# Grouped heads of a two-layer hybrid backbone: the second map is turned behind the first slot of filler, its product comes behind the second

## The chip, the cores and the metric

The kernel runs on one core of a Trainium2 chip. The core has a matrix engine (TensorE; PE in the rows, PEld its weight load), VectorE (DVE), ScalarE (ACT), GpSimd (POOL) and SyncE (SP), which issues the DMAs. Each engine runs its own list of instructions in order and waits at semaphores for the others. The metric is the device time of one execution in microseconds, as the median of several runs.

## The reference

Two layers over 512 latent and 256 context tokens of width 1024. Each layer normalises, projects once into the inputs of three branches, runs them, merges them with gates and adds a gated feed-forward block. What matters here is branch A, attention with eight query heads and two key heads:

```
def gqa_attend(q, k, v):
    s = jnp.einsum('bqkgd,btkd->bkgqt', q * ATTN_SCALE, k).astype(jnp.float32)
    p = jax.nn.softmax(s, axis=-1).astype(v.dtype)
    return jnp.einsum('bkgqt,btkd->bqkgd', p, v)
```

Latent queries attend to all 768 keys (context and latent), context queries to the 256 context keys alone. Branch B is differential attention with four heads (two softmax maps, one subtracted from the other), branch C a convolution. In the second layer only the latent queries are needed.

## The kernel before, in words

**Numbers.** Every value that enters a matrix product is split into a high part, rounded for the matrix engine, and a low part, the rest. A product is three matmuls (high by high, high by low, low by high; L477, L478, L479). ScalarE writes the high part, VectorE (or, for weights, GpSimd) the low one.

**Heads and items.** Attention runs over eight "heads": j = 0 to 3 are grouped heads, each a pair of two query heads, whose two softmax maps lie side by side; j = 4 to 7 are the differential heads. A head runs over query tiles of 128 rows: six in layer 0 (four latent ones with 768 keys, then two context ones with 256 keys), four in layer 1. One query tile of one head is an item, g; `i` is its number within the head.

**What an item does.** `scores` (L576, matmuls at L586) writes the two maps to `sco0` and `sco1`. VectorE takes each map's maximum (`maximum`, L1224, into NM). ScalarE takes the exponential into M with the row sum (`exp`, `ACTIVATE M<-sco,NM`). VectorE scales by the reciprocal of the sum (`gqa_probs`, L1243 and L1244). TensorE turns the probabilities with transposes (`turn_probs`, L599), three blocks of 128 at a time, into the two PSUM banks `aux0` and `aux1`; a context item needs one bank for each map. ScalarE copies the high part out of the bank (`turned_hi`, `ACTIVATE RB<-aux`), VectorE the low part (`turned_lo`, L1181 `RB<-aux,RB`), and only with the latter is the bank free again. `weigh` (L603) is the product with the values for both maps together, 18 matmuls for 768 keys into the bank `acc1`; ScalarE copies the result out (`ACTIVATE X<-acc`, two of 64 rows).

**Filler.** Between these steps TensorE works on the input projection of the next head, in chunks of three matmuls (L477 to L479, `acc<-H,WHI` and `WLO`) into the bank `acc0`; eight chunks make one tile of 384 columns (layer 0) or 512 (layer 1). Each item has two slots of filler, `slot(j, 2 * i)` and `slot(j, 2 * i + 1)`. The table FILL (L47) says how many chunks each slot holds:

```
    (0, "gqa"): [3, 3, 2, 3, 3, 2, 3, 3, 2, 3, 2, 3],
    (1, "gqa"): [4, 4, 2, 2, 1, 1, 1, 1],
    (0, "diff"): [8, 4, 4, 8, 4, 4, 8, 4, 4, 8, 4, 4],
    (1, "diff"): [8, 8, 8, 4, 4, 8, 4, 4],
```

The kind is that of the next head, so head 3 runs with the "diff" rows. To a slot belongs more than the chunks. Where a tile ends in it, ScalarE evacuates the bank in its own slot of the same number (`ACTIVATE M<-acc` or `U<-acc`), and with the last tile of a kind it also splits the next weight tile (`hi`, L788). Some slots later come the sums of squares of each head row (`head_sums`, L564, which also use the two aux banks), their logarithm and exponential on ScalarE (`ACTIVATE R<-aux`, `R<-R`), the rotation on VectorE (`rope`, L1190 and three L1181), its scaling (`normed`), and the split of the new queries and keys (`normed_hi`, `normed_lo`).

**What sets the order.** The order is written out by hand in three loops over the items, one for each engine: TensorE's at L619, ScalarE's at L883, VectorE's at L1273. The three agree in which slot a piece of work falls. The scores of item g+1 are issued right behind the first turn of item g, so that its softmax runs on VectorE and ScalarE while TensorE does the rest of item g.

Of the kernel before, what the change touches and what calls it, by code (L numbers as in the profile page):

```python
# [26 lines left out]
P = 128  # L27
# [102 lines left out]
def build(nc, xT, vecs, consts, wdw, w_mod, w_in, w_gate, w_br, w_out, w_fi, w_fo, out):  # L130
    x_next = nc.dram_tensor("x_next", (P, KC, LAT), F32).ap()

    with ExitStack() as ctx:
# [302 lines left out]
        def _(pe):  # L436
# [139 lines left out]
            def scores(l, g, j, q, k0):  # L576

                kv = kv_buffer(j)
                u = c.at("sc")
                pe.wait_ge(S("exp"), u)  # L580
                pe.wait_ge(S("qk"), qk_count(l, j))
                for a, w, o in ([(0, LAT, 0), (LAT, CTX, LAT)] if k0 == 0 else [(LAT, CTX, 0)]):
                    for n, (x, y) in enumerate(((0, 0), (0, 1), (1, 0))):
                        for m in range(2):
                            h = slice(m * HEAD, m * HEAD + HEAD)
                            mm = nc.tensor.matmul(sco[m][:, o:o + w], QB[h, j % 2, x, q:q + P], KB[h, kv, y, a:a + w],  # L586
                                                  start=n == 0, stop=n == 2)
                            if n == 2 and (k0 or a):
                                mm.then_inc(S(f"scored{m}"), 1)
                c.step("sc")  # L590
# [28 lines left out]
            def attention(l):  # L619
                items = attention_items(l)  # L620
                n = n_tok(l)
                parts = lambda k0: 2 if k0 == 0 else 1

                def project(j):
                    for t, rngs in next_tiles(l, j):
                        yield from tile_chunks((l, j, t), rngs)

                def slot(j, s):
                    if j + 1 == HEADS:
                        return  # L630
                    for _ in range(FILL[l, kind_of(j + 1)][s]):
                        next(chunks)
                    ends = last_slots(l, j + 1)
                    uses = lambda t: [at[(l, j + 1, t), r] for r in range(len(dict(next_tiles(l, j + 1))[t]))]
                    if s == ends["q"] + 1:
                        head_sums(0, n, (l, j + 1, "qs"), uses("q"))
                    if j + 1 >= 4 and s == ends["k"] + 1:
                        head_sums(1, TOK, (l, j + 1, "ks"), uses("k"))
                    if j + 1 >= 4 and s == ends["v"] + 1:
                        turn_v((l, j + 1, "vt"), uses("v"))  # L640

                scores(l, 0, *items[0][0:1], *items[0][2:4])
                for g, (j, i, q, k0) in enumerate(items):
                    if i == 0 and j + 1 < HEADS:
                        chunks = project(j + 1)
                    after = items[g + 1] if g + 1 < len(items) else None
                    turn_probs((l, g, 0), 2 * (g % 2), k0)
                    if after:
                        scores(l, g + 1, after[0], after[2], after[3])
                    if j < 4:  # L650
                        turn_probs((l, g, 1), 2 * (g % 2) + 1, k0)
                    slot(j, 2 * i)
                    if g and items[g - 1][0] >= 4 and items[g - 1][1] % 2:
                        sub_sums((l, g - 1, "ss"), at[l, g - 1, "o"])
                    if i == 0:
                        wait_free("aux", *(at[(l, 0 if j < 4 else j, "vt"), a] for a in range(2)))
                    if j < 4:
                        weigh((l, g, "o"), j, k0, [at[(l, g, m), p] for m in range(2) for p in range(parts(k0))])
                    elif i % 2:
                        weigh((l, g, "o"), j, k0, [at[(l, e, 0), p] for e in (g - 1, g) for p in range(parts(k0))])  # L660
                    slot(j, 2 * i + 1)
                sub_sums((l, g, "ss"), at[l, g, "o"])
                at["attention", l] = dict(c.n)

# [91 lines left out]
        def _(act):  # L756
# [126 lines left out]
            def attention(l):  # L883
# [45 lines left out]
                for g, (j, i, q, k0) in enumerate(items):  # L929
                    after = items[g + 1] if g + 1 < len(items) else None  # L930
                    turned_hi((l, g, 0), 0 if j < 4 else P * (i % 2), k0)
                    if j < 4:
                        turned_hi((l, g, 1), P, k0)
                    if after:
                        exp(0, g + 1, after[3])
                        exp(1, g + 1, after[3])
                        if after[0] >= 4:
                            weighted(g + 1, after[3])
                    slot(j + 1, 2 * i)
                    if j < 4:  # L940
                        b = take(at[l, g, "o"])
                        for m in range(2):
                            rows = slice(m * HEAD, m * HEAD + HEAD)
                            fn(X[rows, j, q:q + P], acc[b][rows, m * P:(m + 1) * P], ACT.Copy,
                               sem=f"acc_free{b}" if m else "oraw")
                    elif i % 2:
                        b = take(at[l, g, "o"])
                        fn(X[:, j, q - P:q + P], acc[b][:, 0:256], ACT.Copy, sem="oraw")
                        fn(OSQ, acc[b][:, 0:256], ACT.Square, sem=f"acc_free{b}")
                    if g and items[g - 1][0] >= 4 and items[g - 1][1] % 2:  # L950
                        sub_factor(l, g - 1)
                    slot(j + 1, 2 * i + 1)
                sub_factor(l, g)
                c.n.update((k, at["attention", l][k]) for k in ("acc", "aux"))

# [209 lines left out]
        def _(dve):  # L1165
# [107 lines left out]
            def attention(l):  # L1273
# [28 lines left out]
                for g, (j, i, q, k0) in enumerate(items):  # L1302
                    after = items[g + 1] if g + 1 < len(items) else None
                    turned_lo((l, g, 0), 0 if j < 4 else P * (i % 2), k0)
                    if after:
                        maximum(0, g + 1, after[3])
                    if j < 4:
                        turned_lo((l, g, 1), P, k0)
                    if after:
                        maximum(1, g + 1, after[3])  # L1310
                    if after and after[0] < 4:
                        gqa_probs(g + 1, after[3])
                    elif after:
                        diff_factors(l, g + 1)
                    slot(j + 1, 2 * i)
                    if after and after[0] >= 4:
                        diff_probs(g + 1, after[3])
                    if g and items[g - 1][0] >= 4 and items[g - 1][1] % 2:
                        sub_norm(l, g - 1, items[g - 1][0], items[g - 1][2])
                    slot(j + 1, 2 * i + 1)  # L1320
# [335 lines left out]
```

## Time and profile before

| | us |
|---|---|
| median of 3 runs (lowest, highest) | 2765.39 (2762.3, 2768.44) |
| the profiled execution | 2768.71 |
| its span | 2766.8 |
| TensorE busy | 2485.3 (90%) |
| VectorE, ScalarE, GpSimd busy | 1214.9, 1150.5, 1019.4 |

Times in the rows are microseconds from the start of the span. A row of the timeline gives start, duration, engine, line and operation, the tile written and those read, the shape and a count; behind it, in brackets, for how long the engine had been idle and what released it. Neighbouring instructions of one kind are merged into one row, with the count. A row of the stretches gives, for each engine, busy time and number of instructions, then the granted clock of TensorE (1.00 is 2.4 GHz, 0.50 is 1.2 GHz), the DMA engines' share and GB/s.

### The profile page before, as it was taken

Reading aid. Unit: us, or ns where it says so; the run is one execution under the profiler, and the core shown is the slowest. Engines: PE = TensorE matmul, PEld = TensorE weight load, DVE = VectorE, ACT = ScalarE, POOL = GpSimd, SP = SyncE. Lnnn points to the kernel's source line nnn. Section 1 sums busy time; section 2 is a strip of 40 time slices with the busy share of each in tenths; the row PEclk is TensorE's granted clock in tenths of the full one; section 3 lists DMA queues with packets and bytes.
Section 4 is the critical chain, followed back from the end, with each engine's and each line's share of the span. In section 5 each row is a group of like instructions: output and inputs, shape, how many; then the busy total and the mean of one; then the engine's idle time right before and its main releaser. Section 6 shows DMA issues by size and latency. Waiting matters only on the chain.

```text
span 2766.8 us, 34285 instructions
## 1 busy us (share of the span) xinstructions
PE 2485.3 (90%) x13556; PEld 2211.2 (80%) x13556; DVE 1214.9 (44%) x1810; ACT 1150.5 (42%) x2256; POOL 1019.4 (37%) x771
## 2 busy tenths in 40 slices
PE   5999888789988998999999998888877869899998
PEld 2888777679987997999999996777666657688887
DVE  3566555578994233111111125764457982311111
ACT  4555566643334335322331226655653233432222
POOL 1201111058883533544552232111113535444443
PEclk9999999889998998999999998999988989999999
DMA  5100111023332422332332121111101214233332
GB/s 203 51 24 24 31 31 39 12 72 120 119 116 80 163 77 69 107 99 77 115 101 68 58 73 61 31 31 38 39 16 54 84 50 133 78 98 99 99 92 91
DMA packets 62077, 209.02 MB, mean 76 GB/s; under 512 B 7392, under 2 KB 7648, under 8 KB 61664
## 3 DMA queue, kind: packets, MB, share of 16 engines
q1 hardware_dynamic: 61920, 206.84, 23.8%
q8 instruction: 109, 1.79, 0.3%
q14 instruction: 48, 0.39, 0.0%
HBM read 202.62 MB, written 4.19 MB: 75 GB/s over the span
## 4 chain that ended last, share of the span: by engine, by line
PE 45%; DVE 10%; ACT 5%; issue 1%; POOL 0%; ACTq 0%; DVEq 0%
PE acc L477 14%; PE acc L478 14%; PE acc L479 14%; DVE X L1491 5%; ACT M L792 2%; DVE M L1181 2%; DVE RB L1181 1%; PE sco L536 1%; PE aux L599 1%; ACT H L792 1%; DVE NM L1224 1%; ACT WHI L788 1%; PE sco L586 1%; ACT RB L792 1%; ACT R L792 0%
## 5 line engine op out<-in xcount | busy, mean ns | idle before, releaser
L401 POOL TENSOR_TENSOR WLO<-STG,WHI 128x512 fp32r<-128x512 f32 (+1 forms) x760 | 1015.4, 1362 | 1724.2 <-ACT WHI L788 1724.1
L477 PE MATMUL acc<-H,WHI 128*128 128x384 f32 (+2 forms) x2528 | 926.3, 366 | 94.8 <-ACT M L792 44.2
L478 PE MATMUL acc<-H,WHI 128*128 128x384 f32 (+2 forms) x2528 | 904.2, 358 | 0.0
L479 PE MATMUL acc<-H,WLO 128*128 128x384 f32 (+2 forms) x2528 | 903.3, 357 | 0.0
L788 ACT ACTIVATE WHI<-STG 128x512 fp32r<-128x512 f32 (+1 forms) x760 | 410.3, 591 | 628.3 <-PE acc L479 405.7
L477 PEld LDWEIGHTS acc<-H,WHI 128*128 128x128 f32 x2528 | 488.8, 193 | 155.7 <-issue 66.6
L479 PEld LDWEIGHTS acc<-H,WLO 128*128 128x128 f32 x2528 | 489.5, 194 | 33.6
L478 PEld LDWEIGHTS acc<-H,WHI 128*128 128x128 f32 x2528 | 490.5, 194 | 30.2
L1491 DVE SCALAR_TENSOR_TENSOR X<-U,WDW,X 128x783 f32<-128x783 f32 (+1 forms) x256 | 336.7, 1315 | 14.8 <-ACT X L792 6.9
L477 PE MATMUL acc<-RB,WHI 128*128 128x384 f32 (+1 forms) x816 | 291.8, 358 | 24.0 <-DVE T L1181 11.2
L1181 DVE TENSOR_TENSOR T<-G,acc 128x384 f32<-128x384 f32 (+1 forms) x114 | 68.2, 599 | 528.2 <-PE acc L479 524.6
L479 PE MATMUL acc<-RB,WLO 128*128 128x384 f32 (+1 forms) x816 | 288.7, 354 | 0.0
L478 PE MATMUL acc<-RB,WHI 128*128 128x384 f32 (+1 forms) x816 | 288.6, 354 | 0.0
L1181 DVE TENSOR_TENSOR RB<-aux,RB 128x384 fp32r<-128x384 f32 (+1 forms) x236 | 119.2, 538 | 228.0 <-ACT RB L792 226.7
L1401 DVE SCALAR_TENSOR_TENSOR X<-acc,MOD,X 128x384 f32<-128x384 f32 (+1 forms) x128 | 67.5, 549 | 320.7 <-PE acc L479 320.7
L477 PEld LDWEIGHTS acc<-RB,WHI 128*128 128x128 f32 x816 | 153.7, 188 | 44.1 <-DVE T L1181 14.1
L792 ACT ACTIVATE M<-sco,NM 128x768 f32<-128x768 f32 (+1 forms) x160 | 129.8, 814 | 85.6 <-DVE NM L1224 85.6
L479 PEld LDWEIGHTS acc<-RB,WLO 128*128 128x128 f32 x816 | 153.8, 188 | 10.9
L599 PE MATMUL aux<-K,M 128*128 128x128 f32 x624 | 101.0, 296 | 68.1 <-DVE M L1257 30.6
L478 PEld LDWEIGHTS acc<-RB,WHI 128*128 128x128 f32 x816 | 153.8, 188 | 10.1
L599 PEld LDWEIGHTS aux<-K,M 128*128 128x128 f32 x624 | 75.7, 150 | 90.9 <-issue 45.1
L792 ACT ACTIVATE RB<-aux 128x384 fp32r<-128x384 f32 (+1 forms) x236 | 102.6, 477 | 102.5 <-PE aux L599 99.8
(112 smaller groups left out, 2352.4 us busy)
## 6 DMA issues: line engine op xcount, KB each, us to landing
STG<-in_w_fi SPq DMA_DIRECT2D x88, 512.0 KB, 3.5
STG<-in_w_mod SPq DMA_DIRECT2D x80, 512.0 KB, 3.5
STG<-in_w_in SPq DMA_DIRECT2D x52, 512.0 KB, 3.5
STG<-in_w_gate SPq DMA_DIRECT2D x48, 512.0 KB, 3.5
STG<-in_w_fo SPq DMA_DIRECT2D x32, 512.0 KB, 3.5
STG<-in_w_br SPq DMA_DIRECT2D x48, 256.0 KB, 2.6
FIRST<-in_w_mod SPq DMA_DIRECT2D x8, 1024.0 KB, 18.6
STG<-in_w_out SPq DMA_DIRECT2D x16, 512.0 KB, 3.6
```

The costliest lines, as they stand in the source:

```text
L401: nc.gpsimd.tensor_tensor(WLO[:, s, a:a + w], STG[:, g, a:a + w], WHI[:, s, a:a + w].bitcast(F32), ALU.subtract).then_inc(S("w_split"), 1)
L477: nc.tensor.matmul(dst, lh, rh, start=first, stop=False)
L478: nc.tensor.matmul(dst, lh, rl, start=False, stop=False)
L479: return nc.tensor.matmul(dst, ll, rh, start=False, stop=last)
L536: mm = nc.tensor.matmul(sco[0][:, row:row + MOD_GROUP], SCX[:, 4 * (4 * q + k):4 * (4 * q + k) + P], w[:, s, k * MOD_GROUP:(k + 1) * MOD_G ...
L586: mm = nc.tensor.matmul(sco[m][:, o:o + w], QB[h, j % 2, x, q:q + P], KB[h, kv, y, a:a + w], start=n == 0, stop=n == 2)
L599: t = nc.tensor.transpose(dst[:, n * P:(n + 1) * P], PR[:, slot, (k - k0) * P:(k - k0 + 1) * P], IDENT)
L788: nc.scalar.activation(WHI[:, s, a:a + w], STG[:, g, a:a + w], ACT.Copy).then_inc(S("w_hi"), 1)
L792: ins = nc.scalar.activation(dst, src, f, **kw)
L1181: return nc.vector.tensor_tensor(dst, a, b, op)
L1401: nc.vector.scalar_tensor_tensor(X[:, j, s:s + m], acc[b][:, s - a:s - a + m], MOD[:, l, part, j, st:st + 1], X[:, j, s:s + m], ALU.mult, ...
L1491: own("tap", nc.vector.scalar_tensor_tensor(o, u, wt, o, ALU.mult, ALU.add))
```

## The change

In the items of heads 0 to 3 each of the three loops is written in another order. On TensorE the second map's turn moves from ahead of the first slot to behind it, the second slot moves ahead of the product. On ScalarE the copies of the second turn move from ahead of the two exponentials to behind the first slot's work, and the copy of the product's result moves behind the second slot's. On VectorE the low parts of the second turn move from between the two maxima to behind the scaling of the next item's probabilities and the first slot's work. Differential heads keep their order.

```
@@ TensorE, attention
                     turn_probs((l, g, 0), 2 * (g % 2), k0)
                     if after:
                         scores(l, g + 1, after[0], after[2], after[3])
+                    slot(j, 2 * i)
                     if j < 4:
                         turn_probs((l, g, 1), 2 * (g % 2) + 1, k0)
-                    slot(j, 2 * i)
+                        slot(j, 2 * i + 1)
...
                         weigh((l, g, "o"), j, k0, [at[(l, e, 0), p] for e in (g - 1, g) for p in range(parts(k0))])
-                    slot(j, 2 * i + 1)
+                    if j >= 4:
+                        slot(j, 2 * i + 1)
@@ ScalarE, attention
                     turned_hi((l, g, 0), 0 if j < 4 else P * (i % 2), k0)
-                    if j < 4:
-                        turned_hi((l, g, 1), P, k0)
                     if after:
                         exp(0, g + 1, after[3])
                         exp(1, g + 1, after[3])
...
                     slot(j + 1, 2 * i)
                     if j < 4:
+                        turned_hi((l, g, 1), P, k0)
+                        slot(j + 1, 2 * i + 1)
                         b = take(at[l, g, "o"])
...
-                    slot(j + 1, 2 * i + 1)
+                    if j >= 4:
+                        slot(j + 1, 2 * i + 1)
@@ VectorE, attention
                     turned_lo((l, g, 0), 0 if j < 4 else P * (i % 2), k0)
                     if after:
                         maximum(0, g + 1, after[3])
-                    if j < 4:
-                        turned_lo((l, g, 1), P, k0)
                     if after:
                         maximum(1, g + 1, after[3])
...
                     slot(j + 1, 2 * i)
+                    if j < 4:
+                        turned_lo((l, g, 1), P, k0)
                     if after and after[0] >= 4:
                         diff_probs(g + 1, after[3])
```

TensorE's list at item 2 of a head of layer 1, before; `aux<-K,M` are the turns, `sco<-RB` the next item's scores, `acc<-H` filler, `acc<-RB` the product:

```order
L599 MATMUL aux<-K,M 128x128 x6
L586 MATMUL sco<-RB 128x512 x6
L586 MATMUL sco<-RB 128x256 x6
L599 MATMUL aux<-K,M 128x128 x6
L477 MATMUL acc<-H,WHI 128x512
L478 MATMUL acc<-H,WHI 128x512
L479 MATMUL acc<-H,WLO 128x512
L477 MATMUL acc<-RB 128x256
```

The same place now:

```order
L599 MATMUL aux<-K,M 128x128 x6
L586 MATMUL sco<-RB 128x512 x6
L586 MATMUL sco<-RB 128x256 x6
L477 MATMUL acc<-H,WHI 128x512
L478 MATMUL acc<-H,WHI 128x512
L479 MATMUL acc<-H,WLO 128x512
L599 MATMUL aux<-K,M 128x128 x6
L477 MATMUL acc<-H,WHI 128x512
L478 MATMUL acc<-H,WHI 128x512
L479 MATMUL acc<-H,WLO 128x512
L477 MATMUL acc<-RB 128x256
```

The second turn has one slot on either side, and the product follows the second slot.

ScalarE's list at items 2 and 3 of head 0 of layer 0, before; `RB<-aux` are the copies of turned blocks (two for each map), `M,L<-sco,NM` the exponentials, `X<-acc` the product's result, `WHI<-STG` the weight split:

```order
L792 ACTIVATE RB<-aux 128x3x128 x4
L792 ACTIVATE M,L<-sco,NM 128x768 x2
L792 ACTIVATE X<-acc 64x128 x2
L792 ACTIVATE M<-acc,EC,V 128x384
L792 ACTIVATE M<-acc 128x384
L788 ACTIVATE WHI<-STG 128x512 x2
L792 ACTIVATE RB<-aux 128x3x128 x4
```

The same place now:

```order
L794 ACTIVATE RB<-aux 128x3x128 x2
L794 ACTIVATE M,L<-sco,NM 128x768 x2
L794 ACTIVATE RB<-aux 128x3x128 x2
L794 ACTIVATE M<-acc,EC,V 128x384
L794 ACTIVATE M<-acc 128x384
L790 ACTIVATE WHI<-STG 128x512 x2
L794 ACTIVATE X<-acc 64x128 x2
L794 ACTIVATE RB<-aux 128x3x128 x2
```

The four copies have become two ahead of the exponentials and two behind them, and `X<-acc` stands last in its item.

VectorE's list over one item with 768 keys on both sides, before; `RB<-aux,RB` are the low parts, `NM<-sco` the maxima, `M<-M,RL` the scalings:

```order
L1181 TENSOR_TENSOR RB<-aux,RB 128x3x128 x2
L1224 TENSOR_REDUCE NM<-sco 128x1
L1181 TENSOR_TENSOR RB<-aux,RB 128x3x128 x2
L1224 TENSOR_REDUCE NM<-sco 128x1
L1243 RECIPROCAL RL<-L 128x1
L1244 TENSOR_SCALAR M<-M,RL 128x768
L1243 RECIPROCAL RL<-L 128x1
L1244 TENSOR_SCALAR M<-M,RL 128x768
```

The same place now, with the item behind it:

```order
L1227 TENSOR_REDUCE NM<-sco 128x1 x2
L1246 RECIPROCAL RL<-L 128x1
L1247 TENSOR_SCALAR M<-M,RL 128x768
L1246 RECIPROCAL RL<-L 128x1
L1247 TENSOR_SCALAR M<-M,RL 128x768
L1184 TENSOR_TENSOR RB<-aux,RB 128x3x128 x4
L1227 TENSOR_REDUCE NM<-sco 128x1 x2
```

The low parts of the second turn now come behind both scalings, next to the first two of the item that follows.

## Rows read from the trace of the kernel before

**Rows 1.** The page, busy time of each engine

```profile
PE 2485.3 (90%) x13556; PEld 2211.2 (80%) x13556; DVE 1214.9 (44%) x1810; ACT 1150.5 (42%) x2256; POOL 1019.4 (37%) x771
```

**Rows 2.** Stretches, heads 0 to 2 of layer 0 and layer 1; PEclk before the DMA columns

```profile
108.85:253.64 144.79, 131.63 (x901) 116.73 (x901) 92.36 (x191) 84.47 (x209) 12.49 (x10) 0.98 0.07 23
1714.00:1823.84 109.84, 97.73 (x654) 82.22 (x655) 74.17 (x141) 64.95 (x149) 12.53 (x10) 0.98 0.09 28
```

**Rows 3.** Waits of TensorE, heads 0-3: layer 0, then layer 1; total, times, longest

```profile
PE aux L599 <- DVE RB L1181: 11.8, 8, 2.0
...
PE aux L599 <- DVE RB L1181: 10.1, 11, 1.6
PE acc L477 <- DVE RB L1181: 4.7, 6, 0.8
```

**Rows 4.** Stretches, items of head 2 of layer 0, then of head 1 of layer 1

```profile
206.09:215.21 9.12, 8.22 (x62) 7.47 (x60) 5.44 (x11) 5.66 (x14) 2.51 (x2) 1.00 0.17 57
215.21:223.89 8.68, 7.98 (x59) 7.00 (x58) 5.34 (x10) 4.98 (x12) 0.00 (x0) 1.00 0.01 2
223.89:231.54 7.65, 7.65 (x59) 6.99 (x57) 5.34 (x10) 4.16 (x10) 0.00 (x0) 1.00 0.00 0
231.54:242.29 10.75, 8.71 (x59) 7.72 (x58) 7.25 (x16) 7.32 (x17) 2.49 (x2) 1.00 0.16 51
242.29:248.24 5.95, 4.90 (x33) 4.13 (x32) 3.41 (x9) 3.33 (x10) 0.00 (x0) 1.00 0.00 0
248.24:253.64 5.40, 5.40 (x39) 4.64 (x37) 3.77 (x8) 3.18 (x8) 0.00 (x0) 1.00 0.00 0
...
1750.66:1762.10 11.44, 10.50 (x67) 8.87 (x66) 5.15 (x10) 5.76 (x14) 2.51 (x2) 1.00 0.16 48
1762.10:1772.28 10.18, 8.63 (x60) 7.37 (x59) 6.83 (x14) 7.72 (x17) 2.50 (x2) 1.00 0.17 52
1772.28:1779.94 7.66, 6.60 (x49) 5.40 (x48) 7.18 (x14) 4.63 (x11) 0.00 (x0) 1.00 0.00 0
1779.94:1787.24 7.30, 6.49 (x50) 5.42 (x49) 5.48 (x11) 4.16 (x11) 0.00 (x0) 1.00 0.01 2
```

**Rows 5.** Timeline, item 2 of head 1 of layer 0, three engines

```profile
174.88 0.82 PE L599 MATMUL aux<-K,M 128*128 128x128 f32 x6
...
175.93 1.02 DVE L1181 TENSOR_TENSOR RB<-aux,RB 128x384 fp32r<-128x384 f32 x2 [2.87 <-ACT RB L792]
...
176.87 0.88 PE L599 MATMUL aux<-K,M 128*128 128x128 f32 x6
176.98 0.96 DVE L1224 TENSOR_REDUCE NM<-sco 128x1 f32<-128x768 f32 x1
...
178.22 0.91 ACT L792 ACTIVATE M<-sco,NM 128x768 f32<-128x768 f32 x1
...
179.26 0.36 PE L477 MATMUL acc<-RB 128*128 128x256 f32 x1
...
179.97 0.62 DVE L1244 TENSOR_SCALAR M<-M,RL 128x768 f32<-128x768 f32 x1
...
181.69 0.57 ACT L792 ACTIVATE X<-acc 64x128 f32<-64x128 f32 x2 [0.79 <-PE acc L479]
```

**Rows 6.** Timeline, work of the slots: evacuation, rotation, head sums, key split

```profile
172.11 0.66 ACT L792 ACTIVATE M<-acc,EC,V 128x384 f32<-128x384 f32 x1
...
190.00 0.72 DVE L1190 STREAM_SHUFFLE G<-M 128x512 f32<-128x512 f32 x1
190.63 1.23 ACT L792 ACTIVATE R<-aux,EC 128x384 f32<-128x384 f32 x2 [1.13 <-PE aux L564]
...
1779.40 0.68 DVE L1181 TENSOR_TENSOR RB<-M,RB 128x512 fp32r<-128x512 f32 x1
```

**Rows 7.** Stretches, behind two idle times of 2.04 us in layer 0

```profile
138.00:140.00 2.00, 2.00 (x8) 2.00 (x7) 1.79 (x6) 1.27 (x5) 0.00 (x0) 0.51 0.63 162
236.50:239.00 2.50, 2.50 (x14) 1.97 (x13) 2.26 (x9) 1.66 (x6) 0.00 (x0) 1.00 0.66 216
```

More of the change, by code:

```diff
@@ L649, in attention @@
                         scores(l, g + 1, after[0], after[2], after[3])
+                    slot(j, 2 * i)
                     if j < 4:
                         turn_probs((l, g, 1), 2 * (g % 2) + 1, k0)
-                    slot(j, 2 * i)
+                        slot(j, 2 * i + 1)
                     if g and items[g - 1][0] >= 4 and items[g - 1][1] % 2:
@@ L660, in attention @@
                         weigh((l, g, "o"), j, k0, [at[(l, e, 0), p] for e in (g - 1, g) for p in range(parts(k0))])
-                    slot(j, 2 * i + 1)
+                    if j >= 4:
+                        slot(j, 2 * i + 1)
                 sub_sums((l, g, "ss"), at[l, g, "o"])
@@ L931, in attention @@
                     turned_hi((l, g, 0), 0 if j < 4 else P * (i % 2), k0)
-                    if j < 4:
-                        turned_hi((l, g, 1), P, k0)
                     if after:
@@ L940, in attention @@
                     if j < 4:
+                        turned_hi((l, g, 1), P, k0)
+                        slot(j + 1, 2 * i + 1)
                         b = take(at[l, g, "o"])
@@ L951, in attention @@
                         sub_factor(l, g - 1)
-                    slot(j + 1, 2 * i + 1)
+                    if j >= 4:
+                        slot(j + 1, 2 * i + 1)
                 sub_factor(l, g)
@@ L1306, in attention @@
                         maximum(0, g + 1, after[3])
-                    if j < 4:
-                        turned_lo((l, g, 1), P, k0)
                     if after:
@@ L1315, in attention @@
                     slot(j + 1, 2 * i)
+                    if j < 4:
+                        turned_lo((l, g, 1), P, k0)
                     if after and after[0] >= 4:
```

## The prediction, made before the result was known

> **What bounds the kernel now.** TensorE has work in 90% of the span [rows 1], and the page's clock row stands at 8 to 9 tenths nearly throughout, so I read the change as a question about TensorE's idle time in the grouped heads and nothing else. The order of views was: the page, then the time by stretches to find these heads, then the waits of TensorE inside them, then one item in order of time.
>
> The change touches heads 0 to 3 of both layers. Heads 0 to 2 take 144.79 us in layer 0 and 109.84 us in layer 1 [rows 2]; head 3, whose filler is that of a differential head, comes on top. In layer 0's grouped heads TensorE waits 11.8 us at the turns for VectorE's split of the turned probabilities, in layer 1's 10.1 us there and 4.7 us at the product for the same kind of split [rows 3]. The first two, 21.9 us in all, are the prize: the second turn needs the two aux banks that the first turn has filled. The reader should see in [rows 4] that not every item pays them: the third item of a layer 0 head takes 7.65 us and TensorE is busy for 7.65 of them, while item 0 of that head holds 0.90 of idle time (9.12 less 8.22) and item 3 holds 2.04 (10.75 less 8.71).
>
> I number items of a head from 0 (six in layer 0, four in layer 1), and count time from the start of an item's first turn.
>
> **What the item does before.** From [rows 5], for item 2 of layer 0: first turn 0, VectorE's two splits 1.05 to 2.07, second turn 1.99 (so the scores of the next item end there), first maximum 2.10 to 3.06, first exponential 3.34, product 4.38, first scaling of the next item's probabilities 5.09 to 5.71, the product's result copied from 6.81 (0.20 behind the product's end at 6.61), next first turn 7.65. Two things matter. The product starts 2.39 us behind the second turn. And ScalarE's copy and VectorE's split of the second turn lie ahead of the exponentials, so nothing but two splits stands between turn and product.
>
> **The change part by part.** Nothing is added or taken away: the same matmuls, copies and splits run. Three orders change.
>
> 1. TensorE: filler, second turn, filler, product, where it was second turn, filler, product, filler. The wait for the aux banks goes: at 1.99 + 1.6 for three chunks the first split (2.07) is long over. Worth up to 21.9 us.
>
> 2. ScalarE: the copy of the second turn now stands behind both exponentials and behind the first slot's work. 3. VectorE: its split stands behind both maxima, both reciprocals and scalings and the first slot's work. Both engines run their list in order (in [rows 5] the exponential starts at 178.22, 0.28 behind the end of its maximum: the copies of the second turn stand ahead of it), so the product now waits for the softmax of the next item, which it does not need.
>
> The chain with the durations of [rows 5], for an item with no extra work in its first slot. The copy of the product's result (0.57 us, at the product's end plus 0.20) now stands directly ahead of the next first turn's copy, which costs that one 0.2. So: splits 1.25 to 2.27; maxima back to back, 2.30 and 3.17, ready 3.26 and 4.12; exponentials 3.29 and 4.18 (0.89 apart, as ScalarE issues them); copies of the second turn from 5.07, first half done 5.55; VectorE scaling 5.40 to 6.02, then the splits 5.94 to 6.96; product 7.2 (0.26 from a split's end to a matmul); product 2.23 long; next first turn 9.4. TensorE itself would be there after 1.99 + 2.39 + 1.04 = 5.4 us, so it waits 1.8. The chain is as long whatever the filler is, so each item now lasts max(chain, TensorE's work).
>
> **Layer 0, heads 0 to 2**, against the undisturbed head in [rows 4]:
> - item 0: chain 9.4 against 9.12, +0.3 (its 0.90 of idle time goes, 1.3 come)
> - item 1: the evacuation of a tile, 0.9 us of ScalarE (two instructions, the first in [rows 6]), stands between exponentials and copy, and the second slot waits for that bank; 10.1 against 8.68, +1.4
> - item 2: 9.4 against 7.65, +1.75
> - item 3: short scores for the next item, but the rotary work of 2.78 us (four instructions of about 0.7, the first in [rows 6]) stands ahead of the split, and the second turn now waits for the banks of the head sums (1.23 us of ScalarE, [rows 6]); split ends 8.5, product 8.7, 10.9 against 10.75, +0.2 (the 2.04 of idle time are taken off in this)
> - item 4: the second slot waits for an evacuation which the product used to cover; 6.75 against 5.95, +0.8
> - item 5: scores of the next head's full tile, chain 5.9 + 0.26, product of six matmuls 0.7; 6.9 against 5.40, +1.5
> A head takes 53.5, three 160.5, against 144.79: **+15.7 us**.
>
> **Layer 1, heads 0 to 2** (slots of 4,4,2,2,1,1,1,1 chunks):
> - item 0: TensorE bound, 2.0 + 2.64 + 0.8 + 2.64 + 2.22 = 10.3 against 11.44, -1.1
> - item 1: rotary work ahead of the split, which ends 9.7; 12.2 against 10.18, +2.0
> - item 2: the key split of 0.68 [rows 6] ahead of it; 10.05 against 7.66, +2.4
> - item 3: chain 9.4 against 7.30, +2.1
> A head takes 42.0, three 126.0; the very first item has no wait at its second turn to lose (nothing stands ahead of it) and starts on a slow clock, so its -1.1 falls away: 127.1 against 109.84, **+17.2 us**.
>
> **Head 3 of both layers** has slots of 4 and 8 chunks; there TensorE is the longer side in most items. The stalls at the turn go, an evacuation is exposed in the items where the first slot ends a tile and the product no longer lies between the slots. I put the two heads at -1.6 together; bounds -6 (all stalls go, nothing comes) and +6 (each item pays 0.6).
>
> **TensorE's clock.** This trace shows no item with idle time like the new ones in heads 0 to 2, so I bound it. Of the four idle times of 2.04 us before item 3's second turn in layer 0, three were followed by a stretch at the 1.2 GHz level; the first and the one that was not stand in [rows 7], with a granted clock of 0.51 and 1.00. Two of these lie in the three heads of 144.79 us, which is 2.14 more than three times the 47.55 of the undisturbed head [rows 2, 4], so about 1.1 us each. Behind 1.55 us or less (item 1 of layer 1 holds 10.18 less 8.63) the clock stayed at 1.00 [rows 4]. The new order has two waits of 2 us or more in each of six heads (item 1 and 4 in layer 0; 2 and 3 in layer 1, with 3.7 and 3.1): nothing to 12 x 1.1 = 13 us. Part of a slow stretch falls where TensorE would wait anyway, so I take **+6**.
>
> The Trainium skill ("TensorE: Matmul & The Clock Gate", A second HAM failure mode: psum-queue depth-cycling) says that frequent small idle times between groups of matmuls are enough to make the clock swing. The idle times of 0.90 and 1.55 us with a clock of 1.00 do not bear this out here; by that page the clock term would be above its upper end, which is rival C.
>
> Sum: 15.7 + 17.2 - 1.6 + 6 = +37.3 us. The profiled execution took 2768.7 us (span 2766.8), 3.3 more than the median, so its counterpart would take 2806 and the median 2802.7.
>
> **The rivals.**
> A. Faster: the second turn's copy does not end up behind the exponentials in effect, because filler covers it. Then the 21.9 us of [rows 3] go and nothing comes: 2743.5. For it: these waits are real and the change removes their cause. Against: it decides only where filler from scores to product exceeds 5.2 us; in heads 0 to 2 that holds for one item of ten, item 0 of layer 1. 5%.
> B. Layer 0 breaks even, because its slots of two or three chunks and shorter handovers than mine hide the chain, and only layer 1 pays: 2765.4 + 17 = 2782. For it: my chain leaves TensorE only 1.3 to 1.8 us idle in most layer 0 items, against 3 to 4 in layer 1. Against: durations and handovers are from the same rows. 12%.
> C. The clock falls at every new wait of over 1 us, that is at some 21 of the 30 items of these six heads, and the slow product and turns lie on the chain: 31.3 + 21 x 1.1 = 54, 2820 (2812 to 2832). For it: the three of four. 14%.
> D. No effect: the chain of the product was only moved, and waits swap one for one, 2765. Against: a layer 1 item has 2.4 us of idle to swap and gets over 3. 3%.
>
> **How the numbers follow.** The forecast, 66%, is 2802, its own range 2787 to 2815 (base 24 to 42, clock 0 to 10). The range of 8 in 10 takes in the upper half of B and the lower half of C and leaves A, D and the rest outside: 2780 to 2822. A difference of 0.2%, 5.5 us, is about what a measurement here can tell from none. Slower: 66 + 12 + 14 = 92%. Same: 3%. Faster: 5%.
>
> **What would show it.** Right: the turns wait no longer for VectorE's split in heads 0 to 2 of either layer (0 to 2 us in all, where 21.9 stood); the product waits for it in nearly every item, some 35 to 55 us in all; layer 0's three heads take about 160 us and layer 1's about 127; outside of the grouped heads every stretch is as long as before. The copy of the second turn starts right behind the second exponential. Wrong: a product that starts with the split of the second turn done before the second exponential; items under 8.5 us in items 2 and 3 of layer 1; a total that moved in the differential heads or behind them.

## The result, and the profile after

The changed kernel takes 2815.21 us (median of 4, 2812.24 to 2823.15) against 2765.33 for the kernel before: a ratio of 1.0191, 95% interval 1.0176 to 1.0206, slower by 50 us. The forecast was 2802, the range 2780 to 2822. The profiled execution is the slowest of the four (2823.15, span 2821.2), so its sections add up to 54.4 us over the span before, where the medians differ by 49.9. Two executions timed for the later experiments (6159 us of the kernel before, 9473 us of the last variant) lie far outside of all others and are left out of the ratios.

First the stretches of the trace after, in the columns of [rows 2]: heads 0 to 2 of layer 0, head 3 of layer 0, everything from there to the first turn of layer 1, heads 0 to 2 of layer 1, head 3 of layer 1.

```profile
110.77:273.66 162.89, 136.31 (x900) 119.85 (x901) 92.05 (x191) 84.30 (x211) 13.35 (x11) 0.96 0.07 20
...
273.66:340.10 66.44, 62.17 (x409) 56.26 (x407) 35.91 (x71) 37.59 (x86) 9.45 (x8) 1.00 0.11 33
...
340.10:1729.99 1389.89, 1276.41 (x7337) 1215.41 (x7336) 573.16 (x806) 544.96 (x1040) 609.65 (x442) 0.96 0.26 82
1729.99:1869.73 139.74, 112.25 (x660) 95.45 (x661) 76.43 (x143) 65.81 (x151) 15.12 (x12) 0.87 0.08 25
1869.73:1933.02 63.29, 55.67 (x327) 46.99 (x327) 30.66 (x55) 32.21 (x68) 7.58 (x6) 0.93 0.10 31
```

The same five of the kernel before, cut at the same instructions (the layer 1 stretch of [rows 2] begins 1.6 us behind its first turn, this one begins at it):

```profile
253.64:321.46 67.82, 62.75 (x407) 57.51 (x405) 38.14 (x72) 38.62 (x89) 10.53 (x8) 0.97 0.11 32
...
321.46:1712.39 1390.93, 1279.45 (x7337) 1216.78 (x7337) 574.04 (x807) 545.17 (x1039) 609.41 (x442) 0.96 0.27 82
...
1712.39:1823.84 111.45, 99.34 (x660) 83.50 (x661) 75.10 (x143) 65.48 (x150) 12.53 (x10) 0.97 0.10 29
1823.84:1879.48 55.64, 50.95 (x327) 43.42 (x326) 31.93 (x55) 31.73 (x69) 10.51 (x8) 1.00 0.12 38
```

Layer 0's heads 0 to 2 have 144.79 us in [rows 2]: +18.1. Head 3 of layer 0 is 1.4 shorter, the long middle 1.0 shorter, layer 1's heads 0 to 2 are 28.3 longer and its head 3 is 7.7 longer. The rest, +2.8, lies ahead of the first turn (1.9) and behind the last grouped head (0.9). So nearly all of it is in the grouped heads. Mind the clock column: 0.87 in layer 1 where 0.97 stood. The 111.45 us before hold a first item of 13.16 us with a clock of 0.77; two later runs that begin layer 1 in the order of before took 10.40 us for it. So the 28.3 us may be up to 3 us too small.

The waits of TensorE in these heads (layer 0 from 110.7 to 340, then layer 1 from 1729.99 to 1933.02), to be read against [rows 3]:

```profile
PE acc L477 <- DVE RB L1184: 11.7, 10, 1.6
PE acc L477 <- ACT M L794: 8.8, 6, 2.1
PE acc L477 <- ACT U L794: 5.4, 3, 1.8
PE acc L477 <- issue: 3.9, 4, 1.1
...
PE aux L599 <- DVE RB L1184: 0.3, 1, 0.3
...
PE acc L477 <- DVE RB L1184: 24.0, 9, 3.5
...
PE aux L599 <- ACT R L794: 5.4, 5, 1.7
...
PE aux L599 <- DVE RB L1184: 1.9, 1, 1.9
```

The waits of the turns for VectorE are 0.3 us where layer 0 had 11.8 and 1.9 where layer 1 had 10.1, all in head 3. New in layer 1 are 5.4 us (0.7 before) in which turns wait for ScalarE to free the banks of the head sums. The product (`acc<-RB`, also L477) now waits for VectorE's split: 11.7 us where layer 0 had 1.4, 24.0 where layer 1 had 4.7. The two rows on ScalarE are filler that waits for an evacuation, in items 1 and 4 of layer 0 and in head 3. Three of the four waits called "issue" stand ahead of the product in item 5 of layer 0, 1.14 us each.

One item in order of time, item 2 of head 1 of layer 0, the one of [rows 5], from the first turn at 186.87:

```profile
186.87 0.82 PE L599 MATMUL aux<-K,M 128*128 128x128 f32 x6
187.07 0.57 ACT L794 ACTIVATE X<-acc 64x128 f32<-64x128 f32 x2 [3.35 <-PE acc L479]
...
188.19 1.02 DVE L1184 TENSOR_TENSOR RB<-aux,RB 128x384 fp32r<-128x384 f32 x2 [3.79 <-ACT RB L794]
189.12 1.81 DVE L1227 TENSOR_REDUCE NM<-sco 128x1 f32<-128x768 f32 x2
190.10 0.90 ACT L794 ACTIVATE M<-sco,NM 128x768 f32<-128x768 f32 x1 [1.57 <-DVE NM L1227]
...
190.54 0.82 PE L599 MATMUL aux<-K,M 128*128 128x128 f32 x6
...
191.87 0.86 ACT L794 ACTIVATE RB<-aux 128x384 fp32r<-128x384 f32 x2
...
192.75 1.02 DVE L1184 TENSOR_TENSOR RB<-aux,RB 128x384 fp32r<-128x384 f32 x2
...
194.02 0.36 PE L477 MATMUL acc<-RB 128*128 128x256 f32 x1 [1.60 <-DVE RB L1184]
```

The second turn is issued at 190.54. ScalarE is busy with the exponentials until 191.87, VectorE with the scalings until 192.75, so the copy and the split of that turn follow only then, and the product starts at 194.02, 7.15 us into the item. The prediction had 7.2, with the copy at 5.07 (measured 5.00) and the split at 5.94 (measured 5.88).

### The profile page after: what moved, and what is told of

It reads as the page before. It is cut to its first block, busy times and chain, and to the rows that moved or that the text cites. A ratio compares the mean times of both kernels' runs of the same rounds, so it can differ in the third digit from the quotient of the medians.

```text
span 2821.2 us, 34285 instructions
## 1 busy us (share of the span) xinstructions
PE 2505.0 (89%) x13556; PEld 2226.7 (79%) x13556; DVE 1212.8 (43%) x1810; ACT 1148.6 (41%) x2256; POOL 1019.8 (36%) x771
## 4 chain that ended last, share of the span: by engine, by line
PE 45%; DVE 10%; ACT 6%; issue 1%; ACTq 0%; DVEq 0%
PE acc L477 14%; PE acc L479 14%; PE acc L478 14%; DVE X L1494 5%; ACT M L794 3%; DVE RB L1184 1%; DVE M L1184 1%; PE sco L536 1%; DVE NM L1227 1%; PE aux L599 1%; PE sco L586 1%; ACT H L794 1%; ACT RB L794 1%; ACT R L794 0%; ACT X L794 0%
## 5 line engine op out<-in xcount | busy, mean ns | idle before, releaser
L477 PE MATMUL acc<-H,WHI 128*128 128x384 f32 (+2 forms) x2528 | 930.0, 368 | 108.8 <-ACT M L794 52.5
L477 PEld LDWEIGHTS acc<-H,WHI 128*128 128x128 f32 x2528 | 488.4, 193 | 175.8 <-issue 66.8
L477 PE MATMUL acc<-RB,WHI 128*128 128x384 f32 (+1 forms) x816 | 292.6, 359 | 23.0 <-DVE T L1184 11.2
L477 PEld LDWEIGHTS acc<-RB,WHI 128*128 128x128 f32 x816 | 154.2, 189 | 43.3 <-DVE T L1184 14.2
L479 PEld LDWEIGHTS acc<-RB,WLO 128*128 128x128 f32 x816 | 154.4, 189 | 10.9
L478 PEld LDWEIGHTS acc<-RB,WHI 128*128 128x128 f32 x816 | 154.3, 189 | 10.1
L477 PE MATMUL acc<-RB 128*128 128x256 f32 x312 | 101.9, 327 | 42.4 <-DVE RB L1184 38.5
L794 ACT ACTIVATE RB<-T 128x384 fp32r<-128x384 f32 (+1 forms) x66 | 37.1, 562 | 247.3 <-DVE T L1184 247.3
```

The costliest lines, as they stand in the source:

```text
L477: nc.tensor.matmul(dst, lh, rh, start=first, stop=False)
L478: nc.tensor.matmul(dst, lh, rl, start=False, stop=False)
L479: return nc.tensor.matmul(dst, ll, rh, start=False, stop=last)
L794: ins = nc.scalar.activation(dst, src, f, **kw)
```

## The experiments

Eight kernels ran. Six differ from the kernel before in order alone, two also hold extra matmuls whose results are overwritten. The first three cuts below are shortened to the order of the steps. In those of the last kernels a function returns three values for each item: whether the second turn stands behind the first slot, whether the product stands behind the second (`last`), and where the second turn's copy and split stand (`'old'` as in the kernel before, `'new'` as in the change). In the lists, `turned_hi(g, 1)` is the copy of the second turn of item g, `turned_lo(g, 1)` its split.

### Only the copy and the split moved

```
 ScalarE  turned_hi(g, 0)
-         turned_hi(g, 1)
          exp(0, g + 1); exp(1, g + 1)
+         turned_hi(g, 1)
          slot(j + 1, 2 * i)
 VectorE  turned_lo(g, 0); maximum(0, g + 1)
-         turned_lo(g, 1)
          maximum(1, g + 1); gqa_probs(g + 1)
+         turned_lo(g, 1)
          slot(j + 1, 2 * i)
```

> TensorE's order is that of before (second turn right behind the scores, product between the slots). Only ScalarE's copy and VectorE's split of the second turn are moved: behind both exponentials and both scalings, ahead of the first slot's work. Theory (the product waits for the softmax of the next item, because copy and split stand behind it in ScalarE's and VectorE's lists): slower than before, and slower than the changed kernel, because the second slot no longer stands ahead of the product: per head about +12 us in layer 0 and +9 in layer 1, with the clock's part 2820 to 2860, I say 2840. The wait of the product for VectorE's split rises from 6 us to over 40. Rival (TensorE's own order costs the time: exposed evacuations, the product behind the last slot): no change from before, 2760 to 2775.

Measured: 2864.26 us (2862.29 to 2867.38), ratio 1.0362 (1.0345 to 1.0379): 100 us slower than before, twice the loss of the change, a little above the stated 2860. One item 1 of layer 0, first turn at 182.33:

```profile
184.32 0.88 PE L609 MATMUL aux<-K,M 128*128 128x128 f32 x6
...
187.19 0.87 ACT L819 ACTIVATE RB<-aux 128x384 fp32r<-128x384 f32 x2
188.06 1.02 DVE L1218 TENSOR_TENSOR RB<-aux,RB 128x384 fp32r<-128x384 f32 x2
189.34 0.36 PE L487 MATMUL acc<-RB 128*128 128x256 f32 x1 [3.07 <-DVE RB L1218]
```

The second turn is where it was, at 1.99 us, and the product starts at 7.01 (4.38 before). With TensorE's list untouched, the place of copy and split in the other two lists alone makes the wait. The rival that TensorE's own order makes the whole loss, with no change from before here, does not stand. That the loss is larger than that of the change fits the second slot: it stands behind the product here and hides nothing of the wait, which is 3.07 us in this item and 1.60 in item 2 above. The waits for VectorE at the product sum to 24.8 us in heads 0 to 2 of layer 0 and 24.9 in those of layer 1, within the "over 40" of the expectation.

### Only the product moved

```
 TensorE  slot(j, 2 * i)
+         slot(j, 2 * i + 1)
          weigh(g)
-         slot(j, 2 * i + 1)
 ScalarE  slot(j + 1, 2 * i)
+         slot(j + 1, 2 * i + 1)
          X <- acc
-         slot(j + 1, 2 * i + 1)
```

> Only the product moves, behind the second slot, in heads 0 to 3; the second turn, its copy and its split stay where they were before. Theory: this part of the change costs little; it exposes an evacuation in items 1 and 4 of layer 0 (+2.1 and +0.7 a head) and in head 3, and hides most of the 0.8 us at the product in items 2 and 3 of layer 1 (-4 in all): +8 us against before, 2765 to 2780. Rival (the order of TensorE's list carries the loss of 50 us): 2800 or more.

Measured: 2771.45 us, ratio 1.0025 (1.0014 to 1.0036), inside the 2765 to 2780. The sum hides two parts of opposite sign. Items 0 to 3 of a layer 1 head, and item 1 of a layer 0 head (columns as in [rows 4]):

```profile
1759.89:1770.92 11.03, 10.45 (x69) 8.91 (x67) 5.41 (x11) 6.96 (x16) 2.62 (x3) 1.00 0.16 49
1770.92:1779.53 8.61, 8.61 (x60) 7.43 (x59) 6.83 (x14) 5.89 (x14) 2.43 (x2) 1.00 0.21 61
1779.53:1786.50 6.97, 6.60 (x51) 5.46 (x49) 6.50 (x13) 4.71 (x11) 0.00 (x0) 1.00 0.00 0
1786.50:1793.35 6.85, 6.54 (x50) 5.58 (x49) 5.91 (x12) 4.75 (x12) 0.00 (x0) 1.00 0.01 2
...
169.21:181.50 12.29, 9.26 (x59) 8.43 (x58) 5.15 (x10) 5.12 (x12) 0.00 (x0) 0.86 0.00 1
```

In layer 1 each of the four is shorter than in [rows 4] (11.44, 10.18, 7.66, 7.30), 3.1 us a head where I had expected 1.3. Item 1 gains most, and it had no wait at its product: its gain is the 1.55 us at its second turn. Before, ScalarE's weight split of the second slot stood ahead of the first copy of item 1; now it stands ahead of `X<-acc` and runs while TensorE does the product. In layer 0, item 1 takes 12.29 for 8.68: a tile ends in its first slot, and without the product between the slots the filler waits 3.03 us for the evacuation and then meets the 1.2 GHz level (0.86). Item 4 loses 0.8 to 2.4 us in the same way. In the sum of its trace, heads 0 to 2 of layer 0 take 154.07 us (+9.3), those of layer 1 99.79 (-11.7, of which 2.8 are the first item, which is 10.37 us long here as in the two later runs named above), and the two heads 3 are 4.0 and 3.7 us longer.

### The copy between the exponentials

```
 TensorE  turned and product as in the change; head_sums behind the second turn
 ScalarE  turned_hi(g, 0); exp(0, g + 1); turned_hi(g, 1); exp(1, g + 1)
 VectorE  turned_lo(g, 0); both maxima; turned_lo(g, 1); gqa_probs(g + 1)
```

> TensorE's order is that of the change, but the sums of squares of the first slot stand behind the second turn; ScalarE copies the second turn between the two exponentials, VectorE splits it behind both maxima and ahead of the scalings. Theory: the chain to the product shrinks from 7.2 to about 5.9 us in a full item, so nearly all of the loss goes: about +2 a head in layer 0, -1 in layer 1, 2760 to 2780, I say 2768. Rival (TensorE's order): stays at 2800 to 2815.

Measured: 2796.53 us (2786.7 to 2798.15), ratio 1.0109 (1.0086 to 1.0132). The forecast of 2768 was missed by 28 us, and 2780, its upper end, by 17. The trace, of the fastest of its runs (2786.7), shows where: head 3 of layer 1, a head of layer 1, a head of layer 0, and the filler behind the evacuation in item 1 of the layer 0 head before that one.

```profile
1834.49:1903.00 68.51, 55.57 (x329) 47.01 (x328) 32.15 (x55) 32.16 (x68) 9.42 (x8) 0.93 0.10 31
1761.36:1797.93 36.57, 32.26 (x222) 27.32 (x221) 24.55 (x47) 22.14 (x51) 5.09 (x5) 1.00 0.10 30
210.68:261.95 51.27, 44.24 (x302) 39.79 (x301) 29.88 (x64) 28.33 (x73) 5.06 (x4) 0.97 0.07 21
...
175.09 0.69 PE L487 MATMUL acc<-H,WHI 128*128 128x384 f32 x1 [2.91 <-ACT M L819]
```

The plain layer 1 head is back at 36.57 (36.58 before, 47.26 in the change): with the chain shortened the ten lost microseconds are gone, although TensorE's turn and product stand as in the change. The product still waits in items 2 and 3 (1.6 us each), which items 0 and 1 make good.

In layer 0 little comes back: 51.3 us, where the change has 52.5 at a clock of 1.00 and the kernel before 47.6 to 49.0. Items 0, 2, 3 and 5 give back 0.5 to 1.3 us each, but item 1 takes 12.2 us (8.68 before) and item 4 6.85 (5.95): their second slot waits for the evacuation of a tile, as in the experiment before. So a part of the loss in layer 0 is not the place of copy and split, but the product that no longer stands between the slots.

The rest of the miss is head 3, which I had not worked out: 12.9 us over the 55.64 of before in layer 1 and 4.4 over the 67.82 in layer 0. There tiles end in first slots, and an evacuation that now follows two exponentials and a copy keeps the second slot waiting, for 4.86 us at worst. About 10 us of the 28 lie between this fastest execution and the median and show in no trace.

### The clock: extra matmuls in the waits

```
             def weigh(name, j, k0, turned, warm=0):
...
+                dst = open_acc(1)
+                for _ in range(warm):
+                    nc.tensor.matmul(dst[:, 0:512], H[:, 0, 0, 0:P], H[:, 0, 0, 0:512], start=True, stop=True)
                 wait_free("aux", *turned)
```

> The changed kernel with 7, 12 and 9 extra matmuls of 512 columns ahead of the product in items 1, 2 and 3 of heads 0 to 2 of layer 1, written to the product's own bank, which the product then starts afresh: 1.5, 2.6 and 2.0 us of work that should fit in the waits of 1.9, 3.4 and 2.7 us. Theory (17 us of the loss, beyond the chain, are the clock at 1.2 GHz behind these waits): faster than the changed kernel by 9 to 14 us, items of 12.2, 10.1 and 9.4 us in place of 13.5, 11.8 and 11.2, the granted clock of these heads 0.97 or more in place of 0.87. Rival (the handovers behind a wait are longer than I took them, the clock is a bystander): no faster than the changed kernel, or slower by up to 18 us of added work.

Measured: 2799.9 us (2797.25 to 2803.94) against 2815.21 for the changed kernel: 15 us faster with 84 matmuls more, a little above the 9 to 14 expected. The two were not timed on one call, but both stand against the kernel before: ratios 1.0131 (1.011 to 1.0152) and 1.0191 (1.0176 to 1.0206), whose difference is 17 us. Layer 1's heads 0 to 2, then head 3, then one whole head and one item 1:

```profile
1730.40:1856.58 126.18, 118.21 (x744) 98.30 (x745) 75.56 (x143) 65.49 (x151) 14.99 (x12) 0.99 0.08 26
1856.58:1915.89 59.31, 51.64 (x328) 43.56 (x327) 30.38 (x55) 32.02 (x68) 7.82 (x7) 1.00 0.12 36
...
1773.53:1815.05 41.52, 38.88 (x251) 32.40 (x250) 24.85 (x47) 22.01 (x51) 5.08 (x5) 1.00 0.08 26
1742.39:1754.42 12.03, 10.64 (x68) 8.58 (x66) 8.51 (x16) 5.75 (x14) 2.43 (x2) 1.00 0.15 44
```

The changed kernel has 139.74 us for the first row with a clock of 0.87, this one 126.18 with 0.99. An undisturbed head takes 41.5 us; the prediction's chain gave 42.0. So the chain was right, and the clock makes the 13.6 us between the two (with head 3, 17.6 in these traces, of which that of the changed kernel is the slowest execution; the totals say 15 to 17). In the changed kernel item 2 of head 1 looks like this: the stretch up to the product, the product up to the next first turn, the stretch behind.

```profile
1799.84:1807.63 7.79, 4.43 (x32) 3.35 (x31) 5.85 (x11) 4.57 (x11) 0.00 (x0) 0.94 0.00 0
1807.63:1811.61 3.98, 3.98 (x19) 3.98 (x20) 0.00 (x0) 0.00 (x0) 0.00 (x0) 0.50 0.01 4
1811.61:1815.00 3.39, 3.39 (x21) 2.69 (x21) 1.45 (x3) 1.52 (x4) 0.00 (x0) 0.69 0.00 0
```

The product follows a wait of 3.36 us and takes 3.98 us where it takes 2.23 at a clock of 1.00.

As a control, the same extra matmuls in the kernel before:

> Control: the same extra matmuls (7, 12 and 9 ahead of the product in items 1, 2 and 3 of heads 0 to 2 of layer 1), but in the kernel before, where the product waits 0.8 us at most and the clock of these heads stood at 1.00 but for their start. Theory (the extra matmuls help only where they fill idle time that would bring the clock down): 1.5 + 1.8 + 1.2 us dearer a head, +13.6 us, 2778 (2772 to 2784). Rival (they help by themselves, by whatever they do to the order or the clock): no slower than before.

Measured: 2773.08 us, ratio 1.0038 (1.0017 to 1.0058), slower by 9. Its items 1 to 3 of layer 1 take 11.80, 8.98 and 8.30 us against 10.18, 7.66 and 7.30. That is 3.9 us a head, a little less than the 4.5 us that they last by themselves. Where there is no long wait they cost time, so their gain above comes from the waits that they fill. The rival that they help by themselves does not stand.

### The change in layer 0 alone

```
-    return (True, True, 'new')
+    return (True, True, 'new') if l == 0 else (False, False, 'old')
```

> The change in layer 0 only; layer 1 as before. Theory by the items of the two traces: layer 0 carries 18.1 us in heads 0 to 2 and -1.4 in head 3, layer 1 the other 38: 2780 (2776 to 2786). Rival (what layer 0 does sets the state in which layer 1 runs, such as the clock or the weights' loading): outside of 2772 to 2790.

Measured: 2777.42 us (2776.76 to 2782.75), ratio 1.0053 (1.0037 to 1.007): layer 0 carries 13 us, inside the 2776 to 2786. The items of layer 1 are as in the kernel before (11.44, 10.18, 7.69 and 7.29 us in head 1), so layer 0 does not set the state in which layer 1 runs. That layer 1 carries the other 37 follows by subtraction; it was not changed alone.

### Where the moves pay

```
+    if j < 3:
+        last = i not in (1, 4) if l == 0 else True
+    else:
+        last = i == 2 if l == 0 else i in (1, 3)
+    return (False, last, 'old')
```

> From the run with the product alone moved: it gained 3.1 us a head in layer 1 (33.46 against 36.58) and in items 0, 2, 3 and 5 of layer 0, and lost 3.6 and 1 to 2 us in items 1 and 4 of layer 0, where a tile ends in the first slot. Here the product stands behind the second slot only where it gained (layer 0: items 0, 2, 3, 5 of heads 0 to 2, item 2 of head 3; layer 1: all items of heads 0 to 2, items 1 and 3 of head 3), and second turn, copy and split stay as before everywhere. Theory (the second turn's place is the harmful part, the product's place is good wherever no evacuation lies between the slots): -7 in layer 0, -9 and -2 in layer 1, so 2746 (2740 to 2755), faster than both kernels. Rival (the gains per item are only shifted to the next item): within 5 us of before.

Measured: 2747.36 us (2746.21 to 2753.18), ratio 0.9943 (0.993 to 0.9956): 17 us faster than the kernel before. One head of layer 1 and one of layer 0, 36.58 and 47.55 in the kernel before [rows 4]:

```profile
1742.61:1776.09 33.48, 32.21 (x223) 27.39 (x222) 24.65 (x48) 22.28 (x52) 5.04 (x4) 1.00 0.10 32
203.31:249.18 45.87, 42.53 (x303) 38.26 (x301) 30.33 (x64) 28.63 (x73) 5.02 (x4) 1.00 0.08 24
```

Here `j < 3` are heads 0 to 2, and `i` counts the items of a head. The product's half of the change is a gain in the items of heads 0 to 2 that have no evacuation between the slots: in layer 0's head 2, items 0, 2, 3 and 5 take 8.90, 7.50, 9.54 and 5.17 us against 9.12, 7.65, 10.75 and 5.40 in [rows 4]. The second and third layer 0 head take 45.8 and 45.9 us with a clock of 1.00. How item 1 of a layer 1 head gains is seen in ScalarE's rows around its first turn, here at 1753.64:

```profile
1752.85 1.15 ACT L819 ACTIVATE WHI<-STG 128x512 fp32r<-128x512 f32 x2
1753.88 0.56 ACT L823 ACTIVATE X<-acc 64x128 f32<-64x128 f32 x2
1754.47 0.87 ACT L823 ACTIVATE RB<-aux 128x384 fp32r<-128x384 f32 x2
```

The weight split runs under the product, and the first copy starts 0.83 us behind the first turn. In the kernel before the split stood between them, and the copy started 2.39 us behind it (1764.49, first turn 1762.10).

> As the by-item kernel, and in item 0 of heads 0 to 2 of layer 1 (slots of 4 chunks) also the second turn behind the first slot, with its copy between the exponentials and its split ahead of the scalings. Theory: these items have the filler to cover a chain of 5.9 us, and lose their wait at the turn: 10.4 for 11.0 us, -2 us against the by-item kernel, 2744. Rival (a late turn costs in any item): slower than the by-item kernel by 2 or more.

Measured: 2747.56 us (2744.15 to 2747.93), where 2744 was expected; ratio 0.9934 (0.992 to 0.9948) against 0.9943 for the kernel above, timed on the same chip in the same call. In the trace two of the three items take 10.37 us in place of 11.03, as expected, and the first takes 10.53 for 11.97; 2 us is less than the totals can tell. The late turn is harmless in an item with eight chunks of filler. The run with extra matmuls, whose copy and split stand behind the softmax, has 10.37 us for this item too: there the filler covers the longer chain as well.

## Why the prediction was right, and where its sizes were off

**The cause** was named rightly: ScalarE's copy and VectorE's split of the second turn stand behind the next item's softmax in lists that run in order. Moving these two alone reproduces the wait (7.01 us to the product against the forecast 7.2). Moving them forward again, with TensorE's turn and product left as changed and only the head sums behind the turn, gives the layer 1 head its 36.57 us back. It does not do so in layer 0, where the evacuations in items 1 and 4 keep most of the loss; the prediction had these as well (+1.4 and +0.8), as a second cause. That the waits of 21.9 us at the turns would go was right too, but for 2.2 us in head 3. Among its signs the prediction puts these 21.9 us in heads 0 to 2; they are those of heads 0 to 3, and 15.3 of them lie in heads 0 to 2.

One sign came out in part only. The product was to wait for VectorE's split in nearly every item, 35 to 55 us in all. It does so in 18 of the 30 items of heads 0 to 2, for 34.8 us, and in three more for 3.4 us under the name "issue".

**Layer 0, heads 0 to 2**, forecast +15.7, measured +18.1. The items of head 1, in a clock of 1.00:

```profile
167.40:176.91 9.51, 8.29 (x62) 7.53 (x61) 5.25 (x10) 4.05 (x10) 1.85 (x2) 1.00 0.19 57
176.91:186.87 9.96, 7.83 (x59) 7.04 (x58) 5.34 (x10) 4.99 (x12) 0.00 (x0) 1.00 0.00 1
186.87:196.25 9.38, 7.78 (x60) 7.01 (x59) 5.25 (x10) 6.03 (x14) 1.98 (x2) 1.00 0.01 2
196.25:206.68 10.43, 9.30 (x61) 7.62 (x59) 7.06 (x16) 5.20 (x13) 0.56 (x1) 1.00 0.17 50
206.68:213.25 6.57, 4.78 (x33) 4.21 (x32) 3.32 (x9) 3.33 (x10) 0.00 (x0) 1.00 0.00 0
213.25:219.86 6.61, 5.47 (x39) 4.71 (x38) 4.15 (x8) 4.64 (x12) 0.68 (x1) 1.00 0.01 2
```

Forecast were 9.4, 10.1, 9.4, 10.9, 6.75 and 6.9. The sum is 52.46 against 53.5, so the part that is there at full clock is 3 x 52.46 - 144.79 = +12.6; the other 5.5 are slow stretches, most of it in head 0, with a clock of 0.91. These vary between executions: in the traces of the run with extra matmuls and of the run with layer 0 alone, whose layer 0 has the same order, the three heads take 158.8 and 161.4 us, which leaves 1.5 and 4.1 for the clock.

**Layer 1, heads 0 to 2**, forecast +17.2, measured +28.3. The part without the clock, from the run with extra matmuls, is 126.18 - 111.45 = +14.7. The forecast of 127.1 us for these heads was nearly met; the +17.2 is 1.6 too large because it was taken against 109.84 us, a stretch that begins 1.6 us behind the first turn.

**Head 3**, forecast -1.6 for both together with bounds -6 and +6. Measured are -1.4 in layer 0 and +7.7 in layer 1, together +6.3, just outside of the bounds. Of the 7.7, 4.0 are the clock (59.31 us in the run with extra matmuls in the heads ahead, 63.29 without). The 3.7 that remain at a clock of 1.00 are an evacuation in item 2 that is no longer covered (filler waits 2.99 us) and a second turn in item 3 that waits 1.94 us for VectorE (0.67 before).

**TensorE's clock** is the term of the sum that was mis-sized. Forecast +6, bound 13; measured 13.6 in layer 1's heads 0 to 2, 5.5 in layer 0's and 4.0 in head 3 of layer 1, 23 in the profiled execution, the slowest of four. Three things were wrong in it. First, the price of 1.1 us for a slow stretch, read from the total of three heads. The two slow items themselves say 1.6 and 1.5 over the 10.75 of [rows 4]:

```profile
133.40:145.74 12.34, 10.30 (x59) 8.96 (x58) 7.24 (x16) 7.30 (x17) 2.50 (x2) 0.86 0.15 44
182.53:194.74 12.21, 10.17 (x60) 9.26 (x59) 7.32 (x16) 7.40 (x17) 2.49 (x2) 0.86 0.13 44
```

The total hid a part of this, because item 0 of the first head has no wait at its second turn and is 0.9 us shorter. Second, in layer 1 the product itself, which lies on the chain, runs behind the wait: item 2 takes 11.77 against 9.86 with the clock held, 1.9 more. Third, I counted waits of 2 us or more and left out item 1 of layer 1, whose waits of 1.16 and 1.89 us at the turn and the product together were followed by the low level in two heads of three (13.54 us with a clock of 0.88 in head 1, against 12.03; in head 0 the same waits left 12.14 us and 1.00).

**How near the rivals came.** The 2815.21 us lie inside the range of 2780 to 2822, but at the very end of the forecast's own range (2787 to 2815), and inside that of rival C (2812 to 2832). C added 54 us to the execution before; the profiled execution has 54.4 us more. So the total is nearer to C's price (2820), which had 14%, than to the forecast, which had 66%, and that it lies in the stated range is in part luck. C's rule was too strong all the same: in layer 0 all six items of head 1 kept 1.00 with waits up to 2.13 us. What brought C's sum about is that slow stretches in layer 1 were dearer than its 1.1 us each (1.9 in item 2). In the forecast the errors offset each other in part: the items of heads 0 to 2 came out 5.6 us below it, while the clock was 17 above and head 3, without the clock, 4 above.

The page on the clock gate in the Trainium skill ("TensorE: Matmul & The Clock Gate", A second HAM failure mode: psum-queue depth-cycling) speaks of swings from small idle times between groups of matmuls. Layer 1 agrees with it (0.86 to 0.89 in every head, with waits of 1.2 to 3.5 us), layer 0's head 1 (1.00, with waits up to 2.13 us) does not.

**Not forecast at all**: that the product's half of the change, alone, would gain 3.1 us a head in layer 1. The prediction priced each item of the whole change and never asked what one of the two moves is worth without the other.

## What to carry to other kernels

Before an operation is moved later on one engine to wait for a buffer, write down the other engines' lists for the same step: if its consumers' work must stand behind something that the path does not need (here two exponentials and two scalings), the wait comes back longer at the next consumer. Price a change that adds idle time to the matrix engine twice, once for the idle time and once for the matmuls behind it at the lower clock; extra matmuls in the wait are a cheap test of the second part. And when a change joins two moves, time them apart: here both together lost 50 us, while the product's move alone, kept where it gained, made the kernel 17 us faster than it was. The late turn, with its copy and split behind the softmax but the product left in its old place, was not timed.

## What the runs showed of the hardware

Waits of 3.3 to 3.5 us in layer 1 were followed each time by a granted clock of 0.50 to 0.58 under the product, while 2.13 us in layer 0 were followed by 1.00 in one head (item 1 of 9.96 us) and by a slow stretch in the two others (11.44 us), with the same instructions. In item 1 of layer 1 a wait of 1.89 us ahead of the product was followed by 1.00 in one head and by 0.56 in the next. Nothing here shows what decides between the two. Filling such waits with matmuls of no use took a stretch from a granted clock of 0.87 to 0.99 and 13.6 us off it; the same matmuls in the kernel before, whose waits are short, cost 9 us.
